# z and o of a gated mixer block in seven half-size block products in place of eight

## What is computed

```python
h = rms_norm(x, norm_g) * (1.0 + scale) + shift        # 4096 x 1024
proj = h @ w_in                                        # u, z_pool, q, k, v, o, z: 512 columns each, 8 gates
pool_out = causal_pool_mixer(u, w_pool, ls_pool) * silu(z_pool)
q, k = split(silu(causal_depthwise_conv(proj[q, k])))
o_gate = sigmoid(proj[..., OFF_O:OFF_ZM])
hm = mlstm_chunkwise(q, k, v, ig, lf)                  # 4 heads, chunks of 128 tokens
hm = hm * rsqrt(mean(hm * hm) + EPS) * mh_norm_g
mlstm_out = hm * o_gate * silu(z_mlstm)
x = x + gate * (concat([pool_out, mlstm_out]) @ w_out)
return rms_norm(x, final_g)
```

## Time and profile before

| | |
|---|---|
| median of 3 runs | 1789.74 us (1789.57 to 1789.86) |
| span of the profiled execution | 1789.0 us |
| PE busy | 1756.0 us, 98% |
| DVE busy | 1073.0 us, 60% |
| ACT busy | 607.4 us, 34% |
| POOL busy | 223.9 us, 13% |
| DMA, mean | 206 GB/s |

### The profile page before, as it was taken

How to read it: one execution, slowest core, us unless ns; L and a number is a source line. 1 busy time by engine, 2 the same in 40 slices (tenths; PEclk the granted TensorE clock), 3 DMA queues, 4 the chain that set the end, 5 groups by cost and what they waited for, 6 DMA issues and landing times.

```text
span 1789.0 us, 24951 instructions
## 1 busy us (share of the span) xinstructions
PE 1756.0 (98%) x9089; PEld 1502.8 (84%) x9089; DVE 1073.0 (60%) x2239; ACT 607.4 (34%) x1446; POOL 223.9 (13%) x197
## 2 busy tenths in 40 slices
PE   6999999999999999999999999999999999999998
PEld 5888879888898888988888888888889888898886
DVE  7786684627835388354864359562784627835383
ACT  4445342433423244222433224232352323422221
POOL 0023231130300013000130002200031000300000
PEclk9999999999999999999999999999999999999999
DMA  9997965798468673786648866487755777467652
GB/s 337 333 284 204 271 163 189 188 304 251 117 214 225 198 225 98 235 248 190 191 130 253 232 190 168 173 222 213 229 132 201 211 206 233 116 214 209 184 171 82
DMA packets 392158, 368.32 MB, mean 206 GB/s; under 512 B 256780, under 2 KB 298724, under 8 KB 392036
## 3 DMA queue, kind: packets, MB, share of 16 engines
q1 hardware_dynamic: 376804, 344.04, 64.7%
q10 hardware_dynamic: 15232, 22.69, 4.5%
HBM read 304.59 MB, written 62.06 MB: 205 GB/s over the span
## 4 chain that ended last, share of the span: by engine, by line
PE 73%; DVE 17%; DMA 4%; issue 3%; ACT 2%; SPq 1%; ACTq 0%; DVEq 0%; POOLq 0%; POOL 0%
PE ps_acc L593 20%; PE ps_acc L595 20%; PE ps_acc L594 20%; PE ps_kv L593 2%; PE ps_kv L594 2%; PE ps_kv L595 2%; DMA sb_kT<-hm_kept 1%; DVE sb_oz L1802 1%; DVE sb_shifted L1823 1%; DVE sb_ada_raw L1414 1%; DVE sb_x_res L1900 1%; PE ps_num L593 1%; PE ps_num L595 1%; DMA sb_w_raw<-w_in 1%; PE ps_num L594 1%
## 5 line engine op out<-in xcount | busy, mean ns | idle before, releaser
L593 PE MATMUL ps_acc<-sb_hT_hi,sb_w_split 128*128 128x512 f32 x1536 | 606.1, 395 | 2.2 <-POOL sb_w_split L1266 1.0
L595 PE MATMUL ps_acc<-sb_hT_hi,sb_w_split 128*128 128x512 f32 x1536 | 598.8, 390 | 0.0
L594 PE MATMUL ps_acc<-sb_hT_lo,sb_w_split 128*128 128x512 f32 x1536 | 597.8, 389 | 0.0
L593 PEld LDWEIGHTS ps_acc<-sb_hT_hi,sb_w_split 128*128 128x128 f32 x1536 | 288.6, 188 | 61.8 <-issue 2.0
L595 PEld LDWEIGHTS ps_acc<-sb_hT_hi,sb_w_split 128*128 128x128 f32 x1536 | 288.3, 188 | 61.3
L594 PEld LDWEIGHTS ps_acc<-sb_hT_lo,sb_w_split 128*128 128x128 f32 x1536 | 288.8, 188 | 57.3
L1277 POOL TENSOR_TENSOR sb_h_rs<-sb_h_var,sb_mhalf 128x4 f32<-128x4 f32 x32 | 40.9, 1279 | 1021.7 <-DVE sb_h_var L1770 1021.7
L1667 DVE SCALAR_TENSOR_TENSOR sb_acc_cv<-sb_shifted,sb_par,sb_acc_cv 128x512 f32<-128x512 f32 x96 | 74.6, 777 | 60.9 <-ACT sb_acc_cv L1097 58.4
L1701 DVE TENSOR_TENSOR sb_oz<-sb_tanh,sb_oz 128x512 f32<-128x512 f32 x32 | 22.2, 693 | 140.5 <-ACT sb_tanh L1121 140.5
L593 PE MATMUL ps_acc<-sb_wo_hi,sb_mixm_hi 128*128 128x512 f32 x256 | 102.4, 400 | 3.7 <-DVE sb_x_res L1900 1.8
L593 PE MATMUL ps_acc<-sb_wo_hi,sb_mixp_hi 128*128 128x512 f32 x256 | 101.0, 394 | 0.0
(11 more groups left out here) (243 smaller groups left out, 2941.6 us busy)
## 6 DMA issues: line engine op xcount, KB each, us to landing
sb_w_split<-w_kept SPq DMA_DIRECT2D x328, 512.0 KB, 4.6
sb_w_split<-w_kept SPq DMA_DIRECT2D x56, 520.0 KB, 4.5
w_kept<-sb_w_split SPq DMA_DIRECT2D x40, 512.0 KB, 4.7
sb_x_res<-x SPq DMA_DIRECT2D x34, 512.0 KB, 5.3
sb_w_raw<-w_in SPq DMA_DIRECT2D x64, 256.0 KB, 4.8
out<-sb_qT SPq DMA_DIRECT2D x32, 512.0 KB, 2.9
sb_x_in<-x SPq DMA_DIRECT2D x112, 128.0 KB, 4.1
sb_ada_raw<-w_ada SPq DMA_DIRECT2D x8, 1024.0 KB, 9.6
```

The source lines that it names most:

```text
L593: pe.matmul(dst, st_hi, mv_hi, start=start, stop=False)
L594: pe.matmul(dst, st_hi, mv_lo, start=False, stop=False)
L595: return pe.matmul(dst, st_lo, mv_hi, start=False, stop=stop)
```

## The change

Block 0 stays as it was but for the additions below. In blocks 1 to 7 the 8 tiles of z and o are replaced. z and o are seen as one product of h (512 tokens by 1024 channels) with 1024 columns (z and o), cut in two along each of tokens, channels and columns. Eight products of 256 tokens by 512 channels by 512 columns would make it; the change makes it from seven, four of which read sums of activations and four sums of weights:

- **On PE** (`zo_products`): products 1, 2, 6, 5, 7, 3, 4, each of 4 K-slices by 2 chunks of 128 tokens by 3 matmuls of 512 columns. Activations are stationary, weights move, the result is token-major. Products 6, 7 and 4 add to a bank that already holds one. A unit is one K-slice of one product (256 KB), used by 6 matmuls; there are 28 units (u0 to u27).
- **Weights**: in block 0 POOL makes the four weight sums (`sum_w`, 4 rounds of 4 additions, loaded to and stored from `x_res`, 1 MB each way a round). The units are loaded raw in every block from 1 on, 8 from `w_in`, 16 from `s_kept`, 4 from `w_in`, and are split in every block: 28 high parts on ACT, 18 low parts on POOL (all of u0 to u7 and the odd ones after), 10 on DVE (the even ones from u8). The keeping of z and o in block 1 goes.
- **Activation sums** (`sum_t`, `low_t`, `split_t`): 16 additions on POOL at the start of each block from 1 on, 8 high parts on ACT at t = 3 and t = 4, 8 low parts on POOL.
- **Around it**: z and o are drawn out of the banks by holds (ACT), sums (DVE), tanhs (ACT) and products (DVE), 6, 8, 8 and 8 of 128 x 512. mh_norm_g is multiplied into w_out once. `oz` is used in `head_norm` (4 smaller instructions in place of one), and `m_mixed` goes from block 1 on.
- **Moved**: the key transposes stand directly behind k3 on DVE; `keep_keys` stands behind u12, u13, u14 and u15. `x_in`, `x_res`, `fg`, `mixm` and the row buffers now share memory with the activation sums; so x of the next block is loaded in the u stage, `fg` once a block, and the first `m_row` after product 6. The ring goes over to 5 slots at unit 52 (the first of u), where it was unit 40.

The core of the diff:

```diff
-UNITS = V_UNITS + 2 * 24
-TILE_UNITS = V_UNITS + 32
+QK_END = V_UNITS + 16
+ZO_UNITS = 28
+UNITS = (V_UNITS + 2 * 24, QK_END + ZO_UNITS + 16)
+TILE_UNITS = (V_UNITS + 32, QK_END + ZO_UNITS)
+PRODUCTS = (1, 2, 6, 5, 7, 3, 4)
+ZO_DVE = [u for u in range(8, ZO_UNITS) if u % 2 == 0]
+ZO_POOL = [u for u in range(ZO_UNITS) if u not in ZO_DVE]
+def slot(b, m):
+    return m % RING if m < TILE_UNITS[late(b)] else m % LOW
...
@@ SP, one block @@
+            def late_block(b, last):
+                for m in range(LOW, UNITS[1]):
+                    if QK_END <= m < TILE_UNITS[1]:
+                        load_zo(b, m - QK_END)
                     else:
                         load_w(b, m)
-                    if m in (33, 35, 37, 39) and not first:
-                        keep_keys(b, (m - 33) // 2)
+                    if m in (36, 37, 38, 39):
+                        keep_keys(b, m - 36)
+                    if m == 57 and not last:
                         load_x(b + 1, 0)
                         load_x(b + 1, 1)
+                    if m == 59:
+                        load_fg()
...
@@ PE @@
+                def zo_product(product):
+                    of_t = {4: 3, 5: 0, 6: 1, 7: 2}
+                    dst = {1: zo_x, 2: zo_z, 3: zo_w, 4: zo_x, 5: zo_y, 6: zo_x, 7: zo_x}[product]
+                    for k in range(4):
...
+                        for j in range(2):
...
+                            last = split3(dst[j][:, :], st_hi, st_lo, w_hi[:, s, :], w_lo[:, s, :],
+                                          k == 0 and product not in (4, 6, 7), k == 3, product in (4, 6, 7))
...
-                for t, (name, i) in enumerate(TILES[:16]):
+                for t, (name, i) in enumerate(TILES[:16 if first else 8]):
                     tile(name, i)
...
@@ ACT, behind the second copy of a q or k tile, ahead of its tanh @@
+                        if not first and t in (3, 4):
+                            split_t(b, t - 3)
+                        if not first and t >= 5:
+                            for u in range(2 * (t - 5), 2 * (t - 5) + 2):
+                                split_zo(b, u)
...
@@ POOL @@
+            def sum_t(b, j):
+                t1, t2, t3, t4 = [t_raw[:, n, 1, j, :, :] for n in range(4)]
...
+                token_half(t1, 0, 2 + j)
+                token_half(t3, 1, 2 + j)
+                token_half(t2, 0, j)
+                token_half(t4, 1, j)
...
+                    pool.wait_ge(acc_full, so_far(TASKS, b))
+                    pool.wait_ge(o_ready, b * NC)
+                    for j in range(2):
+                        sum_t(b, j)
+                    for j in range(2):
+                        low_t(b, j)
+                    for u in ZO_POOL:
+                        low_zo(b, u)
```

679 lines of the change are left out of this document (463 added, 216 removed).

## The result

The changed kernel takes **1902.0 us** (median of four runs, 1895.0 to 1910.6) against 1789.8 us: 1.062 times the time before, 95% interval 1.060 to 1.064. So it is slower, as forecast, but 83 us beyond the 1819 forecast and 52 beyond the range. The profiled execution has a span of 1893.2 us against 1789.0: 104.2 us more.

What follows compares the result with a forecast made beforehand. PE, busy 98%, bounds the kernel: 9.1 us of waits a block against 5.4 saved gives +26 us in seven; with 2 for block 0 and 0.7 run against span, 1789.0 becomes 1818, rounded to 1819 us; range 1774 to 1850.

Steps and rivals of the forecast that it cites:

- What bounds the kernel, and what goes: Whole kernel: PE is the bound, busy 98%; 24 matmuls go in each of 7 blocks, 38.1 us in all.
- Turns of POOL and DVE: q and k tiles: SBUF instructions exclude each other, 0.92 us each; m_row comes 6.4 us later, PE waits 2.8 us a block.
- the rival in which POOL holds on to its recorded end: DVE put off to POOL's recorded end: a pair takes 2.05 us, not 1.7; 1846 us; chance 0.06.
- the faster one: Rival: POOL falls mostly into DVE's gaps and the chain's spare time absorbs the rest; 1767 us; chance 0.16.
- Product 2: Low parts of u2 to u5 meet taps at t = 6 and 7; u6 is late, PE waits 4.4 us a block.
- The clock: Rival: after waits, 9 to 18 matmuls a block run at 1.2 GHz, 0.23 us longer each; 1833 to 1847 us; chance 0.13.
- the likeliest case: The forecast's own layout as it stands: 1803 to 1836 us, waits of 7.5 to 12 us a block; chance 0.46.
- SP and DMA at u13 to u20: Products behind the key transfers: SP late with u13 to u16, u17's low part 0.5 us late; PE waits 0.5 us a block.
- The rival for it: Key transfers cost SP 0.8 us each, landings lengthen half a microsecond, u13 to u20 late; 1859 us; chance 0.10.
- x and `fg` in the u stage: Loads moved into the u stage cost nothing: DMA share 0.73, and 1.5 MB more in 58 us stays below full.
- Unit 52: First unit of u: issued only once u26 is used, so it lands late; PE waits 1.4 us a block.
- Block 0: POOL's 16 additions put DVE off up to 15 us; between 0 and 6 us reach PE, 2 taken.

Runs made afterwards that it cites:

- nosum: The changed kernel without the sums of activations (POOL's additions, ACT's high and POOL's low parts of them): 1867.4 us, ratio 1.042.
- dvesum: The changed kernel with all activation sums and their low parts on DVE, in its idle time, in place of POOL: 1867.1 us, ratio 1.042.
- combo: dvesum with the low parts of u0 to u7 also on DVE, plus ring, xspread and keyspread: 1775.6 us, ratio 0.991 to the kernel before.
- before_pool8: The kernel before plus eight unread POOL instructions of two 128x512 SBUF inputs in each of blocks 1 to 7: 1803.6 us, ratio 1.007.
- keyspread: The changed kernel with the four key transfers at units 36, 40, 44, 48 in place of 36 to 39: 1869.7 us, ratio 1.043.
- keysfew: The changed kernel with key transfers of blocks 2 to 7 cut to an eighth of their bytes, same DMAs and place: 1883.3 us.
- xspread: The changed kernel with x loaded in two parts at units 57 and 60, fg at 64 in place of 59: 1879.6 us, ratio 1.049.
- ring: The changed kernel with the slots of a block's last 16 units turned by three places: 1865.7 us, ratio 1.043.
- nowsum: The changed kernel with POOL's 16 weight sums in block 0 left out, loads and stores kept: 1902.5 us.

## Why the prediction was right in its sign and wrong in its size

76 us of the miss are in the table: 104.0 measured in the stages, 27.6 forecast. 35.9 of them come between u8 and the scores (39.4 measured, 3.5 forecast), 21.4 in the u stage, 9.4 in block 0, 4.8 in the out stage, 4.2 between u6 and u8. The other 7 us of the 83 are mostly the distance of the profiled execution to the median.

- **What bounds the kernel, and what goes**: right (single waits of 3.6, 4.3 and 5.4 us in the prologue, which the reading of the waits passed over, are in both kernels). Left alone, the stages agree to tenths with those of the kernel before: v in the changed kernel, q and k in nosum and dvesum, u in combo; 168 matmuls fewer, at the same distance.
- **Turns of POOL and DVE**: right, to the tenth for m_row (6.5 us later for 6.4, 2.8 us of wait). before_pool8 measures a pair at 1.7 us and rules out the rival in which POOL holds on to its recorded end, and the faster one.
- **Product 2**: right in mechanism and sum. The list of waits has 2.0 us a block (14.3 in seven) for the 4.4 of the forecast, but u6 begins 7.2 us late, as forecast. The rest is PE at the lower clock, which passes the same time (1.6 us in six blocks), and slower first matmuls. What was not in the sum is u8, another 0.6 us.
- **The clock**: given as a rival with 0.13, and it came true beside the likeliest case, not in place of it. The matmuls and their price were said well (9 to 18 a block, 0.23 us each; 94 in blocks 1 to 7, some 13 a block, and 0.20 measured). What they cost the kernel was not: behind m_row they only shorten the wait at product 2, so of the 20 us at most 10 are in the time. They are in the stages named above, most of them in product 7, and no further term.
- **SP and DMA at u13 to u20, "PE waits 0.5 us"**: the step that failed. It had SP's issue time nearly right (0.48 us a key DMA; 0.49 to 0.54 measured), and let units land at a usual time; but u17, 4.0 us late behind the keys, lands after 6.4 us. The load took its place in a burst of five units, issued just as ACT issued its two row loads, and neither is in the layout. In place of 3.5 us in seven blocks PE waits 25.9 for u15 to u17, and with the lower clock and the slow first matmuls behind these waits it is 39.4: the largest term. The rival for it (1859 us, 0.10) had the place right and named both halves, but gave SP's issue the larger change and the landings half a microsecond. keyspread shows that the place of the key stores in the queue brings it about, keysfew that about half hangs on their bytes; what makes the landings long stays open.
- **x and `fg` in the u stage, "costed at nothing"**: failed. A mean share of 0.73 over 58 us says nothing of a queue in which nothing else is issued for 14 us. 21.4 us; xspread, which changes the order alone, gets 17.6 of them back.
- **Unit 52**: right (1.4 forecast, 1.1 to 1.4 measured), but only the first of two effects of the new numbering. The second, SP at the end of a block, was not seen: of the 25.3 us by which ring shortens stages 10.4 are the first effect, 14.9 (7.7 in the u stage, 7.2 in the out stage) the second.
- **Block 0**: 11.4 us for "0 to 6": nowsum puts 4.5 to 7.7 of them on the turns with POOL's 16 additions, the whole near the 15 us bound that the forecast had worked out and then cut to 2 because the work seemed covered. DVE had no cover there: busy 21.66 us of 23 in the kernel before from 90 to 113 us.

## What to carry to other kernels

When units get smaller, the cover of a ring gets shorter in time though its slots stay the same: recount it against the delay of the issue plus the longest landing, not the median, and look at what else stands in the same queue and what another queue sends at that moment. A move that looks free by an average (a share of 0.73, an engine 60% busy) is to be checked for its longest row of one kind: eight DMAs in one piece, four sums in a row, eight low parts in two tiles. And here the arithmetic saving was real: 24 matmuls a block stayed saved once the new work was laid into DVE's idle 16.8 us and the transfers were spread, so a slow first result did not decide about the idea.

## What the runs showed of the hardware that was not expected

- After the waits for m_row, alike at 2.8 us, PE ran for about 3 us at a granted clock of 0.50 in six of seven blocks, beginning between 0 and 1.7 us after the wait. In keyspread it was seven of seven, in keysfew two of seven. After 1.33 us (before_pool8) it did not happen, after 1.78 (block 0 of combo, 249.09) it did. The length of the wait is not all of it: 2.51 us (853.89) had such a stretch behind it, 3.15 us (1766.62) had none, nor had 2.86 (1581.94). What else decides was not settled.
- A DMA share says little of GB/s. With key stores in pieces of 128 bytes under way, 0.86 moved 162 GB/s, while in the u stage of the kernel before 0.73 moved 221. It needs no small pieces: from 619 to 623 us, when the keys had landed and ACT's two loads of one row of 2 KB to 128 partitions were under way, 0.89 moved 167 GB/s.
- The issue of one strided DMA of x (128 KB) cost SP 1.8 us in the mean (14.19 for eight), and not less when spread out (8.08 and 9.38 for four each), against 0.5 for a key DMA of 64 KB. It is no fixed price: single ones took from 0.6 to 3.7 us, and four in the out stage of the kernel before 2.99.
- The turns hold for tiny instructions too: a copy of 128x3 took 1.25 us and an addition of 128x4 0.99 beside POOL, 0.16 alone.
